# Experts' gate and up weights in pieces of 8 KB, on one core of Trainium2

## The reference

```
hg = einsum('sd,edh->seh', xs, w_gate)     # w_gate, w_up: [32, 1024, 256]
hu = einsum('sd,edh->seh', xs, w_up)
h  = silu(hg) * hu * gate[..., None]
return einsum('seh,ehd->sd', h, w_down)    # w_down: [32, 256, 1024]
```

## Time and profile before

| | us |
|---|---|
| median of 3 runs (lowest, highest) | 2507.2 (2505.22, 2509.12) |
| profiled execution, its time | 2503.74 |
| profiled execution, its span | 2502.0 |
| mean granted clock | 0.927 |

### The profile page before, as it was taken

How to read it: one execution, slowest core, us unless ns; L and a number is a source line. 1 busy time by engine, 2 the same in 40 slices (tenths; PEclk the granted TensorE clock), 3 DMA queues, 4 the chain that set the end, 5 groups by cost and what they waited for, 6 DMA issues and landing times. The chain is left out here.

```text
span 2502.0 us, 29536 instructions
## 1 busy us (share of the span) xinstructions
PE 2237.3 (89%) x11074; PEld 1629.5 (65%) x11074; DVE 1318.2 (53%) x2300; ACT 858.6 (34%) x1437; POOL 105.3 (4%) x151
## 2 busy tenths in 40 slices
PE   6698998899997899992799989999979998999997
PEld 4487766556766555551677667877757766787776
DVE  2552346856445555553344485953444456777434
ACT  3321233123222565663343232321333334233223
POOL 0000001200000222210000000000000000000000
PEclk8685999999997899996799999999989999999999
DMA  4230432221323899994332212333323222132402
GB/s 143 106 92 2 116 112 63 67 84 61 104 84 135 283 353 348 336 320 167 92 119 69 63 56 68 102 113 101 109 77 113 98 60 64 41 104 85 134 26 110
DMA packets 275291, 299.05 MB, mean 120 GB/s; under 512 B 48845, under 2 KB 247581, under 8 KB 275113
## 3 DMA queue, kind: packets, MB, share of 16 engines
q1 hardware_dynamic: 270026, 288.71, 35.9%
q0 software_dynamic: 5120, 8.40, 1.1%
HBM read 285.75 MB, written 24.69 MB: 124 GB/s over the span
## 5 line engine op out<-in xcount | busy, mean ns | idle before, releaser
L1466 PE MATMUL acc<-x_hi,w_hi 128*128 128x512 f32 x1632 | 682.4, 418 | 22.2 <-DVE w_lo L1419 15.6
L1467 PE MATMUL acc<-x_lo,w_hi 128*128 128x512 f32 x1632 | 646.6, 396 | 0.0
L1468 PE MATMUL acc<-x_hi,w_lo 128*128 128x512 f32 x1632 | 645.8, 396 | 0.0
L1394 ACT CAST w_hi<-raw 128x1024 fp32r<-128x1024 f32 x204 | 212.6, 1043 | 745.9 <-PE acc L1468 695.0
L1419 DVE TENSOR_TENSOR w_lo<-raw,w_hi 128x1024 fp32r<-128x1024 f32 x195 | 238.4, 1224 | 368.3 <-ACT w_hi L1394 361.6
L1466 PEld LDWEIGHTS acc<-x_hi,w_hi 128*128 128x128 f32 x1632 | 312.4, 191 | 109.9 <-issue 28.9
L1467 PEld LDWEIGHTS acc<-x_lo,w_hi 128*128 128x128 f32 x1632 | 312.4, 191 | 77.1 <-issue 14.1
L1468 PEld LDWEIGHTS acc<-x_hi,w_lo 128*128 128x128 f32 x1632 | 311.5, 191 | 70.6
L1476 PE MATMUL br<-y_t,raw_b 128*128 128x512 f32 x448 | 215.7, 604 | 19.6 <-DVE sg L1428 19.6
L1097 DVE TENSOR_TENSOR w_lo<-wgu,w_hi 128x1024 fp32r<-128x1024 f32 x128 | 150.7, 1220 | 126.7 <-ACT w_hi L1056 126.7
L1056 ACT CAST w_hi<-wgu 128x1024 fp32r<-128x1024 f32 x128 | 127.8, 1045 | 109.8 <-DMA wgu<-in_moe_w_up 105.3
(11 more groups left out here) (512 smaller groups left out, 2656.6 us busy)
## 6 DMA issues: line engine op xcount, KB each, us to landing
raw<-in_w_in SPq DMA_DIRECT2D x61, 1024.0 KB, 5.4
raw<-in_w_gate SPq DMA_DIRECT2D x40, 1024.0 KB, 5.1
wgu<-in_moe_w_gate SPq DMA_DIRECT2D x32, 1024.0 KB, 11.5
wgu<-in_moe_w_up SPq DMA_DIRECT2D x32, 1024.0 KB, 14.7
wd<-in_moe_w_down SPq DMA_DIRECT2D x32, 1024.0 KB, 9.5
raw_b<-in_w_branch SPq DMA_DIRECT2D x56, 256.0 KB, 2.6
room<-in_w_out SPq DMA_DIRECT2D x3, 2048.0 KB, 9.1
y_t<-in_w_out SPq DMA_DIRECT2D x3, 2048.0 KB, 10.6
```

Source lines behind the costliest of these rows:

```text
L1394: self.nc.scalar.copy(self.w_hi[:, n % 2], self.weights(n)).then_inc(self.rounded, 1)
L1466: pe.matmul(acc, hi, tile.hi[:, k, :], start=(k == 0), stop=False)
L1467: pe.matmul(acc, hi, tile.lo[:, k, :], start=False, stop=False)
L1468: mm = pe.matmul(acc, lo, tile.hi[:, k, :], start=False, stop=(k == KT - 1))
```

## The change

The rows of gate and up are spread over the partitions in another way: partition p gets rows 8p to 8p + 7, which lie one behind the other in memory, 8 KB. The buffer becomes [128, 3, 2, 8, 256], gate's 8 KB and then up's on each partition. For each k the stationary operand must have the same rows of x, so `turn_x` takes every eighth column of x, from k on, in place of 128 columns in a row. `w_hi` and `w_lo` keep their shape, gate and up side by side; ScalarE and VectorE read a part of `wgu` as four runs of 256 and write it as before. Counts of instructions, waits and bytes stay the same.

```
@@ experts
-        wg, wu = (wgu[:, n].rearrange("p k j -> p (k j)").rearrange("p (u k j) -> p u k j", u=2, k=KT) for n in range(2))
+        wg, wu = (wgu[:, n] for n in range(2))
@@ experts_by_token
         def part(t, p):
-            return t[:, 2 * p:2 * p + 2, :]
+            return t[:, 2 * p:2 * p + 2, :].rearrange("p k (n j) -> p k n j", n=2)
+
+        def raw_part(j, p):
+            return wgu[:, j % SLOTS, :, 2 * p:2 * p + 2, :].rearrange("p n k j -> p k n j")
@@ SP
-                    for dst, src in ((wgu[:, s, :, 0:HID], w_gate), (wgu[:, s, :, HID:], w_up)):
-                        sp.dma_start(dst, src[j].rearrange("(k p) n -> p k n", p=P)).then_inc(gu_in[s], 16)
+                    for n, w in enumerate((w_gate, w_up)):
+                        sp.dma_start(wgu[:, s, n], w[j].rearrange("(p k) n -> p k n", p=P)).then_inc(gu_in[s], 16)
@@ turn_x
-                        mm = pe.transpose(rows_ps[:, k, :], xg[:, j % 2, k * P:(k + 1) * P], c.const("ident", CAP)[:, 0:CAP])
+                        mm = pe.transpose(rows_ps[:, k, :], xg[:, j % 2, k:D:KT], c.const("ident", CAP)[:, 0:CAP])
@@ w_round
-                        nc.scalar.copy(part(w_hi, p), part(wgu[:, j % SLOTS], p)).then_inc(w_rounded, 1)
+                        nc.scalar.copy(part(w_hi, p), raw_part(j, p)).then_inc(w_rounded, 1)
@@ w_rest
-                        nc.vector.tensor_tensor(part(w_lo, p), part(wgu[:, j % SLOTS], p), part(w_hi, p).bitcast(F32),
+                        nc.vector.tensor_tensor(part(w_lo, p), raw_part(j, p), part(w_hi, p).bitcast(F32),
                                                 ALU.subtract).then_inc(w_split, 1)
@@ the block
-        wgu, wd = c.sb(ctx, "wgu", [P, EXPERT_SLOTS, KT, 2 * HID]), c.sb(ctx, "wd", [P, EXPERT_SLOTS, 2, D])
+        wgu, wd = c.sb(ctx, "wgu", [P, EXPERT_SLOTS, 2, KT, HID]), c.sb(ctx, "wd", [P, EXPERT_SLOTS, 2, D])
...
-            c.to_fetch += [(wgu[:, n, :, at:at + HID], w[n].rearrange("(k p) n -> p k n", p=P), gu_in[n])
-                           for at, w in ((0, moe[0]), (HID, moe[1]))]
+            c.to_fetch += [(wgu[:, n, m], w[n].rearrange("(p k) n -> p k n", p=P), gu_in[n]) for m, w in enumerate(moe[0:2])]
```

## The result

| | before | after |
|---|---|---|
| median, us (runs) | 2507.05 (4) | 2491.1 (4) |
| lowest and highest, us | 2505.22, 2509.12 | 2488.98, 2491.96 |
| profiled execution: span, us | 2502.0 | 2488.7 |

The ratio of after to before is 0.9935, with a 95% interval of 0.9918 to 0.9952: 16 us faster, by more than the 5 us that can be told from no change.

What follows compares the result with a forecast made beforehand. The prediction took DMA as the bound of the expert stage, 9.91 us an expert, with PE next at 8.97; 26 periods shortened to 9.10 save 21.1 us, so the median goes from 2507.2 to 2486 us, range 2481 to 2501.

Steps and rivals of the forecast that it cites:

- A: Expert stage: the forecast itself, DMA and PE nearly equal at 8.97 to 9.22 us an expert, 2483 to 2490 us; 48%.
- case B: Turn of x on PE: slower by 0.25 to 0.6 us, eating part of the gain; 2495 us, ends 2490 and 2501; 26%.
- The bound before was DMA, PE next at 8.97 us: Expert stage: transfers set 9.91 us an expert, PE alone 0.94 us less, so faster transfers give at most 24.4 us.
- The DMA term, 9.10 us: Expert stage: with 8 KB runs the transfers of one expert take 9.10 us in place of 9.91.
- The factor of 1.074 over the burst rates: Expert loads: measured period over the sum from short-stretch rates, 9.23 us; applied to 8.46 us after, it gives 9.08.
- Rival C: Expert stage: larger packets bring little when the stage is full; 2507 us without gain in rate, 2500 at 354 GB/s; 16%.
- the 9.52 us: Expert stage: period if HBM's limit of about 358 GB/s for a core held, giving 2497 us.
- The casts and subtractions cost nothing: ScalarE and VectorE: reading four runs of 256 in place of one adds nothing; 0.4 us an expert if cover goes.
- The turn, 0 to 0.13 us: PE's eight transposes an expert: loading x with a step of eight adds 0 to 0.13 us, not showing beside DMA.
- The sum: Whole kernel: 26 x (9.91 - 9.10) = 21.1 us off the profiled execution, median from 2507.2 to 2486 us.
- Rival D: Turn of x on PE: so dear that the kernel gets slower, 11 us at 224 ns a transpose, 2518 us; 10%.
- Room for late transfers: Gate and up loads: 13.6 us of room after issue; landing should come at 10 to 12 us, inside it.

Runs made afterwards that it cites:

- the 1 KB kernel: The kernel before, gate and up loaded in 1 KB runs, with the gate/up matmuls on `w_lo` left out: 2501.4 us, period 10.0 us.
- the 8 KB kernel: The changed kernel with `turn_x` again taking 128 columns in a row, so x and weights are paired wrongly: 2478.8 us, period 8.97 us.

## Why the prediction came out as it did

The range (2481 to 2501) held 2491.1, and faster at 0.81 was right; but the likeliest case, A, was not what happened. The range held the result because it took in case B. The median alone would not say so (2491.1 lies between A's 2486 and B's 2495); the turn and the period do. Step by step:

- *The bound before was DMA, PE next at 8.97 us.* Right, and shown: with half of PE's product left out the 1 KB kernel stayed at 10.0 us, and with the turn undone the 8 KB kernel ran at 8.97. (One reading was off: slice 14 has the DMA digit 8 and 283 GB/s; only slices 15 to 18 are at 9 and over 300. Nothing hangs on it.)
- *The DMA term, 9.10 us.* Right in kind, slightly too long: about 8.9 by itself (8.94 by the issues, 8.88 by the rate). The factor of 1.074 over the burst rates came out as 8.94/8.46 = 1.057. Rival C (a full stage gains no rate) fell at 362, 379 and 384 GB/s. The Trainium skill, "DMA: Bandwidth & Descriptors", Specifications, gives 512 bytes for line rate; these traces do not agree, with 347, 374 and 384 GB/s for gate and up in runs of 1, 2 and 8 KB. Its 358 GB/s for HBM is half of a stack's rate, a share for each of two cores; here, with one core at work, it was passed (384 GB/s), so the 9.52 us that the prediction worked out from it did not hold the stage. The runs grew on both sides of the transfer at once, in memory and on the partitions, so which side's length counts is not shown.
- *The casts and subtractions cost nothing.* Right: 1,047 and 1,220 ns, and behind PE.
- *The turn, 0 to 0.13 us.* This step failed. It was 0.38 us (1.09 against 0.71), with no cover. Case B, priced at 0.40 from the turn at half clock, gave a period of 9.37, and 9.36 was measured. My reason for the low end was that the turn at half clock was only 1.6 times as long, "so the load is not all that fills the 80 ns of a transpose, and a little slowing is hidden". The slowing was not little. The row that I had called nearest gave the size; I argued it away. Its way was not quite that of case B, though: the loads did not go at half rate (200 ns against 141), and with the step the turn takes about the same time at either clock (1.09 us at 1.00, 1.13 at 0.50). That it comes out as long as a turn in a row at half clock (1.11) may be luck; no run tells.
- *The sum.* Between the profiled executions the gain is 13.3 us (2503.74 to 2490.44); B's sum said 12.0, A's 21.1. Its parts were off both ways: counted by `wd` issues the old period was 9.83 and not the 9.91 of the first roundings, so 26 steps gave 12.2 and not 14.0; and the tail was left out, 21.5 us from the last `wd` issue to the last down product before and 19.4 after. The medians differ by 16.0, more than the profiled pair, since the profiled execution was 3.3 us below its median before and 0.7 after; so B's 2495 came out 4 us too high, A's 2486 5 us too low.
- *Rival D* (a turn so dear that the change loses) fell: it would have had to cost 0.94 us, and cost 0.38.
- *Room for late transfers.* Right: up lands 10.8 us after issue, and PE did not wait for it.

That the step of the read is the cause is shown by the kernel that undoes only it. Why a weight load with a step is slower is not shown, nor why steps of two and four cost 0.08 us more than eight.

## What to carry to other kernels

When a stage has a bound and a next bound 10% behind it, cost every part of an edit against the second: what is free while the first holds is paid in full once it is gone. Larger runs for a DMA can ask for a step on the reader's side, as here; look which engine does that read, and let one with time to spare put the data in order, after a look at what else that engine's copy holds up: on VectorE and ScalarE it paid, on POOL it lost most of the gain. A price that no row shows should be taken from the nearest row as it stands, not from what one hopes is hidden.

## What the runs showed of the hardware

- Eight transposes of 64 x 128 take 0.71 us at clock 1.00 with columns in a row, 1.09 with a step of eight, 1.17 with a step of two or four. At clock 0.50 (the turn of expert 0) it is 1.11, 1.13 and, for four and two, 1.22 and 1.21. So the turn with a step is nearly as long at either clock, and a step of eight costs almost nothing at the lower one. The 1.13 is from the changed kernel; its like of before stands in the earlier trace rows:

```profile
819.91 1.13 PE L1001 MATMUL ps<-consts,y 64*128 64x64 f32 x8 [8.43 <-PEq L156]
```

- The Trainium skill, "SBUF — State Buffer", Specifications (TRN2), expects full rate with two hits on a 16-byte line. TensorE's weight load does not agree (a step of two costs as much as four); ScalarE's copy does (2,161 ns with a step of eight, 1,113 with two, and 1,047 for its casts of 1,024 elements in runs of 256). For VectorE no run tells: its copy of 1,024 elements took 1,168 ns with a step of eight, and a copy of 512 elements in a row (`merged` from `sg`) 427.
- A copy on POOL slowed VectorE's subtractions beside it from 1,220 to 1,556 ns in the mean; VectorE's own copy left them at 1,218.
